# The x transposes of a chunked scan, one projection later

## Chip, cores and metric

One core of one Trainium2 chip runs the whole kernel as one program. The metric is device time in microseconds (us) for one execution; the kernel before takes 848.48 us (median of 3 runs, 846.72 to 849.82).

## What is computed

Two layers on 512 positions of width 1024, in float32: a bidirectional Mamba-2 (SSD) layer and a differential attention layer. The change lies in the SSD layer alone. Its scan, cut to what matters, with 8 groups of 4 heads of width 64, state 128, chunks of 128 positions (4 chunks), run forward and on the flipped sequence:

```python
X, B, C = chunks of (x * dt), B, C            # x, B, C: conv + SiLU of the input projection
L = exp(segment sums of dt * A)               # 128 x 128 per head, chunk and direction
y_diag = einsum(C, B, L, X)
states = einsum(B, exp(a_cs[-1] - a_cs), X)   # per chunk
prev   = running sum of states, decayed from chunk to chunk
y_off  = einsum(C, prev, exp(a_cs))
y = y_diag + y_off                            # both directions are summed; then + D * x, times SiLU(z)
```

## The kernel before

Each engine has its own program, written out by hand; they meet in counting semaphores, and each engine runs its own instructions in order. The SSD input projection is cut into units of 128 output channels. Six units (slots 0 to 5) make one iteration: z (two units), x (two units), B and C of one group. A unit is 24 matmuls of 512 columns (8 blocks of the inner dimension, three products each, since weights and activations are split into a high and a low part), made by `project` (L1288) into bank 0 or 1 in turn, so a projection waits for the SiLU of the unit two before it (L1292). Weights come by DMA into a ring of four buffers; ScalarE (ACT) rounds them to the high part (`split_hi`, L595) and GpSimd (POOL) takes the low part (`split_lo`, L469), three units ahead.

While the units of group g+1 are projected, the scan of group g is worked on between them; here "group g" names that iteration, and its steps in each slot are:

- slot 0: PE transposes x into banks 2 and 3 (8 transposes, L1307). ACT runs the tanh of z (L639), copies x to `x_nat` (two copies, L667) and does the exponentials of head 2 (L694). POOL does `split_lo`, then `scale_x_dec` (L487): two products of `x_nat` with the decays into `x_dec` (L493).
- slot 1: PE transposes B into bank 4 (L1317), makes C-by-B into bank 5 (L1320). ACT: tanh of z, copy of B (L685), exponentials of head 3, squares. DVE: SiLU of z (L952), then `pair_weights` (L958) for heads 0 and 1 and again for heads 2 and 3: two sums of rows, both inputs in SBUF (L962), then two products with bank 5 (L966).
- slot 2: PE makes the states from `x_dec` and `B_nat` into banks 4, 2 and 3 (L1331). DVE: convolution of x (L937, four taps), the running states (L976, L982), SiLU. POOL: `split_lo`, then `squares` (L511).
- slot 3: PE makes the diagonal part (L1342) and the part from earlier chunks (L1355). DVE: convolution, the y sums (L997 to L1006) into `x_nat`, SiLU. ACT issues the load of the next rows.
- slots 4 and 5: convolutions of B and C; POOL adds the masks (`mask_rows`, L504) for the next group; PE transposes y (L1362) after slot 5's projection.

PE does its scan work of a slot after that slot's projection. Groups 2 to 5 run in a hardware loop of two trips with two groups each. In the last group there are no units for slots 2 to 5; the first units of the output projection (`out_unit`, L1380) stand there, and DVE does two steps of the gate's low part (`gated_lo`, L1018, L1021; both inputs in SBUF) ahead of the SiLU of slot 1, for which the first `out_unit` waits (L1385).

Of the kernel before, what the change touches and what calls it, by code (L numbers as in the profile page):

```python
# [32 lines left out]
NC = L // P  # L33
# [8 lines left out]
GROUPS = 8  # L42
HPG = HEADS // GROUPS
# [80 lines left out]
def build(nc, x, norm_w, ssd_w_in, ssd_conv_w, ssd_conv_b, ssd_dt_bias, ssd_a_log, ssd_d,  # L124
# [3 lines left out]
    with stack:  # L128
# [202 lines left out]
        def after(eng, s, n):  # L331

            if not (isinstance(n, int) and n <= 0):
                eng.wait_ge(s, n)
# [104 lines left out]
        def _(pool):  # L439
# [74 lines left out]
            def ssd_iteration(m, half, slots=range(SLOTS), scan=True):  # L514
                last_g = isinstance(m, int) and m * 2 + half == GROUPS - 1
                for slot in range(SLOTS):
                    if slot == 0 and last_g:
                        scale_x_dec(GROUPS - 1)
                    if slot in slots:
                        split_lo(ssd_unit(m, half, slot).plus(AHEAD))  # L520
                    if scan and slot == 0 and not last_g:
                        if isinstance(m, int) and m * 2 + half == 0:
                            mask_rows(0, range(HPG))
                        scale_x_dec(m * 2 + half)
                    if scan and slot > 3 and slot in slots:
                        mask_rows(m * 2 + 1 + half, range(2 * slot - 8, 2 * slot - 6))
                    if scan and slot == 2 and not (isinstance(m, int) and m * 2 + half == 0):
                        squares(m * 2 + half - 1)
# [64 lines left out]
        def _(act):  # L593
# [64 lines left out]
                        .then_inc(sq_in, 1)  # L658

            def scan_ops(g, slot, half):  # L660
                if slot == 0:

                    after(act, y_done, g * NC)
                    after(act, yt_done, g * 2)
                    for i in range(2):
                        act.wait_ge(tr_done, g * 4 + i + 1)
                        nc.scalar.copy(x_nat[:, 2 * i:2 * i + 2, :].rearrange("p c w -> p (c w)"),  # L667
                                       bank[2 + i][:, :]).then_inc(x_nat_in, 1)
                last_g = isinstance(g, int) and g == GROUPS - 1
                if slot == 1 and not last_g:  # L670
                    copy_b(g)
                if slot == 2:
                    act.wait_ge(st_done, g * 3 + 1)
                    after(act, off_done, g * NC)
                    nc.scalar.copy(pair(0), bank[scan_banks(g)[0][0]][:, :]).then_inc(prev0_in, 1)
                first = isinstance(g, int) and g == 0
                for r in ((0,) if first else () if last_g else (2,),
                          (1, 2, 3) if first else (2, 3) if last_g else (3,), (), (), (), ())[slot]:
                    exps(g, r)

            def copy_b(g):

# [29 lines left out]
            def ssd_iteration(m, half, slots=range(SLOTS), scan=True):  # L712
                last_g = isinstance(m, int) and m * 2 + half == GROUPS - 1
                for slot in range(SLOTS):
                    if slot == 1 and last_g:
                        copy_b(GROUPS - 1)
                    if slot in slots:
                        split_hi(ssd_unit(m, half, slot).plus(AHEAD))
                        evacuate(m, half, slot)
                    if scan and slot == 5 and slot in slots:  # L720
                        exps(m * 2 + 1 + half, 0)
                    if slot == 1 and last_g:
                        gated_hi(0)
                        gated_hi(1)
                    if scan:
                        scan_ops(m * 2 + half, slot, half)
                    if scan and slot == 1 and not (isinstance(m, int) and m * 2 + half == 0):
                        squares(m * 2 + half - 1)
                    if slot in slots and slot >= 2:
                        tanh(m, half, slot)  # L730
                    if scan and slot == 3 and slot in slots:
                        load_rows(act, m * 2 + 1 + half)
                    if scan and slot == 5 and slot in slots:
                        exps(m * 2 + 1 + half, 1)
# [517 lines left out]
        def _(pe):  # L1252
# [44 lines left out]

            def scan_ops(g, slot, half):
                last_g = isinstance(g, int) and g == GROUPS - 1
                if slot == 0:  # L1300

                    pe.wait_ge(silu_done, g * SLOTS + 2)
                    after(pe, y_done, g * NC)
                    for i in range(2):
                        for c in (2 * i, 2 * i + 1):
                            for j in range(2):
                                ins = T.transpose(bank[2 + i][:, (c % 2) * GW + j * P:(c % 2) * GW + (j + 1) * P],  # L1307
                                                  xT[:, half, j, c * P:(c + 1) * P], ident[:, :])
                        ins.then_inc(tr_done, 1)
                if slot == 1:  # L1310

                    if isinstance(g, int) and g == 0:
                        pe.wait_ge(rows_sb, 1)
                        pe.wait_ge(sp_a, 7)
                    pe.wait_ge(silu_done, g * SLOTS + 4)
                    for c in range(NC):
                        ins = T.transpose(bank[4][:, c * P:(c + 1) * P], BT[:, c * P:(c + 1) * P], ident[:, :])  # L1317
                    ins.then_inc(tr_done, 1)
                    for c in range(NC):
                        ins = T.matmul(bank[5][:, c * P:(c + 1) * P], BT[:, c * P:(c + 1) * P],  # L1320
                                       CTr[:, c * P:(c + 1) * P], start=True, stop=True)
                    ins.then_inc(tr_done, 1)
                if slot == 2:

                    pe.wait_ge(xdec_done, g * 2 + 2)
                    pe.wait_ge(x_nat_in, g * 3 + 3)
                    after(pe, g_done, g * 2)
                    for k in range(3):
                        b = bank[scan_banks(g)[0][k]]
                        for d, (c, i) in enumerate(((k, k), (3 - k, 2 - k))):  # L1330
                            ins = T.matmul(b[:, d * GW:(d + 1) * GW], B_nat[:, c, :], x_dec[:, d, i, :],  # L1331
                                           start=True, stop=True)
                        ins.then_inc(st_done, 1)
                if slot == 3:

                    pe.wait_ge(m_done, g * HPG + HPG)
                    if last_g:
                        pe.wait_ge(prev_done, g + 1)
                    for c in range(NC):
                        for r in range(HPG):  # L1340
                            at = (c % 2) * GW + r * HD
                            ins = T.matmul(bank[6 + c // 2][:, at:at + HD], rows[:, r, c * P:(c + 1) * P],  # L1342
                                           x_nat[:, c, r * HD:(r + 1) * HD], start=True, stop=True)
                        if c % 2:
                            ins.then_inc(diag_done, 1)
                if slot == 3 or slot == 4 and last_g:

                    pe.wait_ge(prev_done, g + 1)
                    for c in (range(NC) if not last_g else range(2) if slot == 3 else range(2, NC)):
                        if slot == 4:  # L1350
                            pe.wait_ge(y_done, g * NC + c - 1)
                        for d in range(2):
                            k = (c - 1, 2 - c)[d]
                            if 0 <= k < 3:
                                ins = T.matmul(bank[scan_banks(g)[1][c]][:, d * GW:(d + 1) * GW], CTr[:, c * P:(c + 1) * P],  # L1355
                                               prev[:, k, d, :], start=True, stop=True)
                        ins.then_inc(off_done, 1)
                if slot == 5:
                    pe.wait_ge(y_done, g * NC + NC)
                    for j in range(2):  # L1360
                        for c in range(NC):
                            ins = T.transpose(bank[6 + j][:, c * P:(c + 1) * P], x_nat[:, c, j * P:(j + 1) * P],  # L1362
                                              ident[:, :])
                        ins.then_inc(yt_done, 1)
# [246 lines left out]
```

## Time and profile before

| | us |
|---|---|
| median of 3 runs | 848.48 |
| the profiled execution | 852.42 |
| its span in the trace | 850.7 |
| PE busy | 787.7 (93%) |
| DVE busy | 538.0 (63%) |
| POOL busy | 456.5 (54%) |
| ACT busy | 405.0 (48%) |
| mean granted TensorE clock | 0.982 of full speed |

All rows and numbers taken from the trace belong to the profiled execution, on a time axis that starts with its span. PE is the matmul side of TensorE, ACT is ScalarE, POOL is GpSimd, DVE is VectorE. Group 0 of the scan begins near 60 us, the following ones near 112, 157, 206, 252, 301, 347 and 392 us; the output projection and the attention layer follow.

### The profile page before, as it was taken

Reading aid. Unit: us, or ns where it says so; the run is one execution under the profiler, and the core shown is the slowest. Engines: PE = TensorE matmul, PEld = TensorE weight load, DVE = VectorE, ACT = ScalarE, POOL = GpSimd, SP = SyncE. Lnnn points to the kernel's source line nnn. Section 1 sums busy time; section 2 is a strip of 40 time slices with the busy share of each in tenths; the row PEclk is TensorE's granted clock in tenths of the full one; section 3 lists DMA queues with packets and bytes.
Section 4 is the critical chain, followed back from the end, with each engine's and each line's share of the span. In section 5 each row is a group of like instructions: output and inputs, shape, how many; then the busy total and the mean of one; then the engine's idle time right before and its main releaser. Section 6 shows DMA issues by size and latency. Waiting matters only on the chain.

```text
span 850.7 us, 11488 instructions
## 1 busy us (share of the span) xinstructions
PE 787.7 (93%) x3824; PEld 639.4 (75%) x3824; DVE 538.0 (63%) x893; ACT 405.0 (48%) x807; POOL 456.5 (54%) x254
## 2 busy tenths in 40 slices
PE   1987999999999899999799999899999999998887
PEld 0766888887878788888687888766777777776576
DVE  4754869596777859596662113367668677676732
ACT  4557273634637282745732134344645454645420
POOL 5438494856667475857545434645545636445111
PEclk9999899999999999999999999999999999999999
DMA  9115524324243424233152332513223132120002
GB/s 263 54 41 166 186 62 125 115 73 159 75 148 99 148 58 152 87 111 113 50 198 76 105 99 62 155 51 96 69 77 97 50 97 91 53 96 25 1 1 99
DMA packets 98804, 82.57 MB, mean 97 GB/s; under 512 B 5152, under 2 KB 87424, under 8 KB 96712
## 3 DMA queue, kind: packets, MB, share of 16 engines
q1 hardware_dynamic: 95760, 66.99, 26.4%
q10 hardware_dynamic: 2904, 15.01, 4.8%
q8 instruction: 24, 0.39, 0.2%
q14 instruction: 20, 0.16, 0.1%
q0 software_dynamic: 96, 0.02, 0.0%
HBM read 79.74 MB, written 2.26 MB: 96 GB/s over the span
## 4 chain that ended last, share of the span: by engine, by line
PE 51%; DVE 21%; issue 11%; POOL 8%; ACT 6%; DMA 1%; DVEq 1%; ACTq 0%; SPq 0%; POOLq 0%
PE bank L1259 42%; DVE c_acc L937 4%; POOL w_lo L472 3%; DVE rows L962 3%; POOL stat L464 2%; ACT ex L790 2%; PE bank L1342 2%; DVE sbias L1126 2%; PE bank L1331 1%; PE bank L1355 1%; POOL rows L504 1%; DVE tmp L997 1%; DVE ex L1137 1%; ACT qkvz L855 1%; ACT w_hi L601 1%
## 5 line engine op out<-in xcount | busy, mean ns | idle before, releaser
L472 POOL TENSOR_TENSOR w_lo<-w_raw,w_hi 128x1024 fp32r<-128x1024 f32 x104 | 260.9, 2510 | 256.4 <-ACT w_hi L601 256.3
L1259 PE MATMUL bank<-hn_hi,w_hi 128*128 128x512 f32 (+1 forms) x392 | 160.1, 408 | 11.1 <-DVE xT L952 7.7
L1259 PE MATMUL bank<-hn_hi,w_lo 128*128 128x512 f32 (+1 forms) x392 | 154.5, 394 | 0.0
L1259 PE MATMUL bank<-hn_lo,w_hi 128*128 128x512 f32 (+1 forms) x392 | 154.3, 394 | 0.0
L601 ACT CAST w_hi<-w_raw 128x1024 fp32r<-128x1024 f32 x104 | 108.8, 1047 | 77.1 <-PE bank L1259 70.7
L1259 PE MATMUL bank<-w_hi,hn_hi 128*128 128x512 f32 x320 | 131.4, 410 | 7.7 <-DVE zT L952 5.0
L1259 PE MATMUL bank<-w_hi,hn_lo 128*128 128x512 f32 x320 | 125.6, 392 | 0.0
L1259 PE MATMUL bank<-w_lo,hn_hi 128*128 128x512 f32 x320 | 125.6, 392 | 0.0
L937 DVE SCALAR_TENSOR_TENSOR c_acc<-bank,par,c_acc 128x510 f32<-128x510 f32 (+1 forms) x128 | 95.8, 748 | 34.1 <-ACT c_acc L643 25.4
L790 ACT ACTIVATE ex<-sbias,stat 128x512 f32<-128x512 f32 x64 | 45.7, 716 | 120.6 <-DVE stat L1130 120.6
L1259 PEld LDWEIGHTS bank<-hn_hi,w_hi 128*128 128x128 f32 (+1 forms) x392 | 74.2, 189 | 29.2 <-issue 14.0
L504 POOL TENSOR_TENSOR rows<-rows,below 128x1024 f32<-128x1024 f32 x32 | 76.5, 2415 | 21.3 <-DMA rows<-acs_rows 21.3
L1259 PEld LDWEIGHTS bank<-hn_hi,w_lo 128*128 128x128 f32 (+1 forms) x392 | 74.0, 189 | 16.7
L1259 PEld LDWEIGHTS bank<-hn_lo,w_hi 128*128 128x128 f32 (+1 forms) x392 | 74.2, 189 | 15.2
L1259 PEld LDWEIGHTS bank<-w_hi,hn_hi 128*128 128x128 f32 x320 | 60.5, 189 | 29.5 <-issue 13.3
L694 ACT ACTIVATE rows<-rows,da 128x128 f32<-128x128 f32 x256 | 78.0, 393 | 3.4 <-POOL rows L504 3.4
L650 ACT ACTIVATE bank<-c_acc 128x512 f32<-128x512 f32 x32 | 19.3, 602 | 115.9 <-DVE c_acc L937 115.9
L1259 PEld LDWEIGHTS bank<-w_hi,hn_lo 128*128 128x128 f32 x320 | 60.4, 189 | 13.3
L1259 PEld LDWEIGHTS bank<-w_lo,hn_hi 128*128 128x128 f32 x320 | 60.7, 190 | 11.0
L1259 PE MATMUL bank<-w_hi,oT_hi 128*128 128x512 f32 x128 | 53.2, 416 | 3.5 <-DVE stat L1130 1.6
L962 DVE TENSOR_TENSOR rows<-rows 128x512 f32<-128x512 f32 x32 | 49.8, 1590 | 3.0 <-ACT rows L694 3.0
L1259 PE MATMUL bank<-w_hi,oT_lo 128*128 128x512 f32 x128 | 51.6, 403 | 0.0
(191 smaller groups left out, 1265.1 us busy)
## 6 DMA issues: line engine op xcount, KB each, us to landing
w_raw<-in_ssd_w_in SPq DMA_DIRECT2D x48, 512.0 KB, 4.0
w_raw<-in_attn_w_in SPq DMA_DIRECT2D x64, 256.0 KB, 3.1
rows<-acs_rows ACTq DMA_DIRECT2D x14, 1024.0 KB, 6.4
w_raw<-in_ssd_w_out SPq DMA_DIRECT2D x16, 512.0 KB, 3.6
w_raw<-in_attn_w_out SPq DMA_DIRECT2D x16, 256.0 KB, 3.1
wbias<-bias_rows SPq DMA_DIRECT2D x8, 448.0 KB, 4.1
rows<-in_x SPq DMA_DIRECT2D x4, 512.0 KB, 5.4
rows<-acs_rows SPq DMA_DIRECT2D x2, 1024.0 KB, 5.9
```

Of the source, the lines that this page charges most:

```text
L464: return nc.gpsimd.tensor_tensor(dst, src, expo[:, 0:n], ALU.pow)
L472: nc.gpsimd.tensor_tensor(w_lo[:, s, :], w_raw[:, s, :], f32(w_hi[:, s, :]), ALU.subtract)\
L504: nc.gpsimd.tensor_tensor(pair_, pair_, below[:, :, :].unsqueeze(2).to_broadcast([P, 2, NC, P]), ALU.add).then_inc(mask_done, 1)
L601: nc.scalar.copy(w_hi[:, s, :], w_raw[:, s, :]).then_inc(hi_done, 1)
L650: nc.scalar.activation(bank[u.c % 2][:, :], c_acc[:, u.c % 2, :], ACT.Tanh).then_inc(tan_done, 1)
L694: ins = nc.scalar.activation(part, part, ACT.Exp, bias=da[:, c, d, ds(g * HPG + r, 1)])
L790: nc.scalar.activation(ex[:, j, :], sbias[:, j, :], ACT.Exp, bias=stat[:, 36 + j:37 + j], accum_out=stat[:, 40 + j:41 + j]).then_inc(e_don ...
L937: ins = V.scalar_tensor_tensor(c_acc[:, p, lo:hi], bank[p][:, lo + sh:hi + sh], par[:, ds(t + (PC_W + k * CT), 1)], c_acc[:, p, lo:hi], AL ...
L962: ins = V.tensor_tensor(rows[:, r, :], rows[:, r, :], rows[:, HPG + r, :], ALU.add)
L1126: ins = V.tensor_tensor_reduce(out=sbias[:, j, :], in0=bank[4 + j][:, :], in1=w, scale=1.0, scalar=-3.0e38, op0=ALU.add, op1=ALU.max, accu ...
L1259: ins = T.matmul(dst, a[i], b[j], start=first and n == 0, stop=last and n == 2)
L1342: ins = T.matmul(bank[6 + c // 2][:, at:at + HD], rows[:, r, c * P:(c + 1) * P], x_nat[:, c, r * HD:(r + 1) * HD], start=True, stop=True)
```

## The change

On PE, the eight x transposes of a group move from after slot 0's projection to after slot 1's projection, ahead of B's transposes. On ACT, the two copies of x move from slot 0 to slot 1, right ahead of the copy of B. On POOL, `scale_x_dec` stands at the beginning of slot 1 for all groups. For groups 0 to 6 that is the same place in POOL's order as before (behind slot 0's `split_lo`, ahead of slot 1's); in the last group it stood ahead of slot 0's `split_lo` and now stands behind it. In the last group ACT's copies of x stand with the copy of B ahead of slot 1's `split_hi` and tanh. No instruction is added or removed.

```diff
@@ POOL, ssd_iteration
-                    if slot == 0 and last_g:
-                        scale_x_dec(GROUPS - 1)
+                    if scan and slot == 1:
+                        scale_x_dec(m * 2 + half)
                     if slot in slots:
                         split_lo(ssd_unit(m, half, slot).plus(AHEAD))
-                    if scan and slot == 0 and not last_g:
-                        if isinstance(m, int) and m * 2 + half == 0:
-                            mask_rows(0, range(HPG))
-                        scale_x_dec(m * 2 + half)
+                    if scan and slot == 0 and isinstance(m, int) and m * 2 + half == 0:
+                        mask_rows(0, range(HPG))
@@ ACT, scan_ops
-                if slot == 0:
-
-                    after(act, y_done, g * NC)
-                    after(act, yt_done, g * 2)
-                    for i in range(2):
-                        act.wait_ge(tr_done, g * 4 + i + 1)
-                        nc.scalar.copy(x_nat[:, 2 * i:2 * i + 2, :].rearrange("p c w -> p (c w)"),
-                                       bank[2 + i][:, :]).then_inc(x_nat_in, 1)
                 if slot == 1 and not last_g:
+                    copy_x(g)
                     copy_b(g)
@@ ACT, new function with the lines removed above
+            def copy_x(g):
@@ ACT, ssd_iteration
                     if slot == 1 and last_g:
+                        copy_x(GROUPS - 1)
                         copy_b(GROUPS - 1)
@@ PE, scan_ops
-                if slot == 0:
+                if slot == 1:
 
                     pe.wait_ge(silu_done, g * SLOTS + 2)
                     after(pe, y_done, g * NC)
```

## Rows read from the trace of the kernel before

**Rows 1.** The page's chain that ended last: shares of the span by engine.
```profile
PE 51%; DVE 21%; issue 11%; POOL 8%; ACT 6%; DMA 1%; DVEq 1%; ACTq 0%; SPq 0%; POOLq 0%
```
**Rows 2.** Timeline of PE, groups 2 and 3: start, duration, engine, line, what [idle before].
```profile
162.88 1.03 PE L1307 MATMUL bank<-ident,xT 128*128 128x128 f32 x8
163.67 0.48 PE L1259 MATMUL bank<-hn_hi,w_hi 128*128 128x512 f32 x1
...
169.22 0.27 PE L1317 MATMUL bank<-ident,BT 128*128 128x128 f32 x1
...
198.03 0.47 PE L1259 MATMUL bank<-hn_hi,w_hi 128*128 128x512 f32 x1 [2.10 <-DVE xT L952]
...
245.90 0.47 PE L1259 MATMUL bank<-hn_hi,w_hi 128*128 128x512 f32 x1 [1.30 <-DVE xT L952]
```
**Rows 3.** Chain that ended last, in order of time: slot 5's projection in group 2.
```profile
198.03 7.31 PE bank L1259 x24
```
**Rows 4.** Busy time by window, columns PE, PEld, DVE, ACT, POOL, clock, DMA, GB/s.
```profile
200.00:202.00 2.00, 2.00 (x6) 1.62 (x5) 1.19 (x3) 0.74 (x2) 2.00 (x2) 0.50 0.01 2
```
**Rows 5.** Timeline of DVE, slot 1 of group 2, up to slot 2's convolution.
```profile
170.65 2.97 DVE L962 TENSOR_TENSOR rows<-rows 128x512 f32<-128x512 f32 x2
173.74 1.28 DVE L966 TENSOR_TENSOR rows<-rows,bank 128x512 f32<-128x512 f32 x2
...
174.95 2.90 DVE L962 TENSOR_TENSOR rows<-rows 128x512 f32<-128x512 f32 x1
...
180.76 0.74 DVE L937 SCALAR_TENSOR_TENSOR c_acc<-bank,par,c_acc 128x510 f32<-128x510 f32 x1
```
**Rows 6.** Timeline of DVE, the same stretch of group 3.
```profile
219.69 3.02 DVE L962 TENSOR_TENSOR rows<-rows 128x512 f32<-128x512 f32 x2
222.74 1.28 DVE L966 TENSOR_TENSOR rows<-rows,bank 128x512 f32<-128x512 f32 x2
...
223.94 0.68 DVE L962 TENSOR_TENSOR rows<-rows 128x512 f32<-128x512 f32 x1
...
228.62 0.74 DVE L937 SCALAR_TENSOR_TENSOR c_acc<-bank,par,c_acc 128x510 f32<-128x510 f32 x1
```
**Rows 7.** Timeline of POOL in slots 1 and 2 of groups 2 and 3.
```profile
170.08 2.39 POOL L472 TENSOR_TENSOR w_lo<-w_raw,w_hi 128x1024 fp32r<-128x1024 f32 x1
174.92 2.37 POOL L472 TENSOR_TENSOR w_lo<-w_raw,w_hi 128x1024 fp32r<-128x1024 f32 x1 [2.46 <-ACT w_hi L601]
...
223.94 2.90 POOL L472 TENSOR_TENSOR w_lo<-w_raw,w_hi 128x1024 fp32r<-128x1024 f32 x1 [2.39 <-ACT w_hi L601]
```
**Rows 8.** Timeline of ACT, tanh of slot 1 in group 3.
```profile
218.46 0.59 ACT L639 ACTIVATE c_tan<-bank 128x512 f32<-128x512 f32 x1
```
**Rows 9.** Timeline of ACT, slot 0 of the last group.
```profile
399.75 0.58 ACT L639 ACTIVATE c_tan<-bank 128x512 f32<-128x512 f32 x1
400.24 1.05 ACT L667 COPY x_nat<-bank 128x512 f32<-128x512 f32 x2
```
**Rows 10.** Timeline of POOL, slots 0 and 1 of the last group.
```profile
401.36 2.91 POOL L493 TENSOR_TENSOR x_dec<-x_nat,xdw 128x768 f32<-128x768 f32 x2 [1.69 <-ACT x_nat L667]
404.22 4.84 POOL L472 TENSOR_TENSOR w_lo<-w_raw,w_hi 128x1024 fp32r<-128x1024 f32 x2
```
**Rows 11.** Timeline of DVE in group 0, while POOL goes over to x_dec.
```profile
79.02 1.30 DVE L962 TENSOR_TENSOR rows<-rows 128x512 f32<-128x512 f32 x1 [1.51 <-ACT rows L694]
...
81.55 0.68 DVE L962 TENSOR_TENSOR rows<-rows 128x512 f32<-128x512 f32 x1
```
**Rows 12.** Timeline of POOL in group 0, the second x_dec product.
```profile
81.61 1.95 POOL L493 TENSOR_TENSOR x_dec<-x_nat,xdw 128x768 f32<-128x768 f32 x1
```
**Rows 13.** Timeline of DVE, slot 1 of the last group.
```profile
407.78 2.50 DVE L1021 SCALAR_TENSOR_TENSOR hn_lo<-gT,par,hn_hi 128x512 fp32r<-128x512 f32 x2 [6.73 <-ACT hn_hi L709]
```
**Rows 14.** Timeline of PE, first unit of the output projection.
```profile
410.93 0.80 PE L1259 MATMUL bank<-w_hi,hn_hi 128*128 128x512 f32 x1 [4.96 <-DVE zT L952]
```
**Rows 15.** Timeline of PE in group 0, the states.
```profile
83.62 0.79 PE L1331 MATMUL bank<-x_dec,B_nat 128*128 128x256 f32 x1 [3.75 <-POOL x_dec L493]
```

More of the change, by code:

```diff
@@ L679, in scan_ops @@
                     exps(g, r)
+            def copy_x(g):
+                after(act, y_done, g * NC)
+                after(act, yt_done, g * 2)
+                for i in range(2):
+                    act.wait_ge(tr_done, g * 4 + i + 1)
+                    nc.scalar.copy(x_nat[:, 2 * i:2 * i + 2, :].rearrange("p c w -> p (c w)"),
+                                   bank[2 + i][:, :]).then_inc(x_nat_in, 1)
             def copy_b(g):
```

## Prediction

> **What bounds the kernel now.** I read the page's chain first: PE carries half of it and DVE a fifth [rows 1]. In the SSD stage PE is nearly always busy, so the next question is where it isn't. The PE timeline answers: slot 5's projection waits for DVE's SiLU of x in the loop's groups, 2.10 us in group 2 and 1.30 in group 3 [rows 2]. The pattern repeats: groups 4 and 5 wait about 2.4 and 1.3; groups 1 and 6 wait next to nothing. A wait of 2.1 costs more than itself. The projection behind it has 7.31 us on the chain [rows 3], while an undisturbed one takes 169.22 - 163.67 = 5.55 [rows 2], and two microseconds after it began the granted clock is 0.50, the lower level of 1.2 GHz [rows 4]. After the wait of 1.30 no such stretch shows. I price the drop at 1.6 us (7.16 us to the next PE step less 5.55). So the even groups lose about 4 us each, the odd ones 1.3. PE further waits 3.75 us for `x_dec` in group 0 [rows 15] and 4.96 us for the SiLU of z in the last group [rows 14].
>
> Why is that SiLU late? DVE works without a break from the row sums of slot 1 on. A sum takes 0.68 us when it runs alone [rows 6], yet in group 2 the first two take 2.97 and the next 2.90 [rows 5]. The POOL timeline beside it shows why: `split_lo` runs from 170.08 to 172.47, and at 174.92, 0.03 us ahead of DVE's sum at 174.95 [rows 5, 7]. A sum with both inputs in SBUF thus stands still until POOL's running instruction is over, and ends 0.55 us later (170.65 + 2.97 less the second sum's 0.60 is 173.02, against 172.47). In group 3 both start at 223.94, DVE goes first in 0.68 us, and POOL's instruction stretches from 2.39 to 2.90 [rows 6, 7]. Whoever is first wins, and that is the difference between the even and the odd groups. From the first sum to slot 2's convolution: 180.76 - 170.65 = 10.11 us in group 2, 228.62 - 219.69 = 8.93 in group 3 [rows 5, 6].
>
> **PE, part by part.** The eight transposes take 163.67 - 162.88 = 0.79 us [rows 2] wherever they stand; PE's total is unchanged. But slot 1's projection now starts and ends 0.79 earlier. States need the products one projection (5.55 us) plus B and C-by-B later; POOL needs some 4.5 us, so no wait there. Slot 1's projection loses 0.79 us of slack on slot 5's SiLU of C; by my reading of the timelines 0.15 us is left in groups 3 to 5, so I take zero, and at most 0.2 us per group as a risk.
>
> **ACT.** Two copies take 1.05 us, 0.94 to the next start [rows 9]. In groups 3 to 5 the tanh of slot 1 shows no idle time ahead of it [rows 8]: ACT is late, not PE. Without the copies it starts 0.94 earlier; in groups 1 and 2 PE sets it, 0.79 earlier. In slot 1 the copies stand ahead of B's copy and head 3's exponentials, which end about 0.2 us later than now; DVE wants head 3 only with its fourth sum, three microseconds after that. Queued behind are the squares and slot 2's `split_hi`, whose reader POOL is busy anyway. No DMA of the ring is due within 15 us of it.
>
> **POOL and DVE: the race.** Count from slot 1's tanh, t = 0. Its SiLU ends such that the first sum starts at 1.22 (219.69 - 218.46) [rows 6, 8]. In the last group the copies follow the tanh at 0.49 and POOL starts `x_dec` at 1.61 [rows 9, 10]; I use that spacing. POOL meanwhile has nothing: its slot 0 `split_lo` is over, and the other waits behind `scale_x_dec`. So:
> - Sum 1 runs free, 1.22 to 1.90. POOL starts `x_dec` at 1.61, ahead of sum 2 (due at 1.82). One `x_dec` alone takes 1.46 [rows 10]; begun beside sum 1, about 1.6, so it ends at X = 3.2, and sum 2 ends at X + 0.55.
> - The two products follow after 0.03 (group 3) or 0.12 (group 2: 173.74 - 173.62) and take 1.20 [rows 5, 6]. Sum 3 is due at X + 1.78 in odd groups, X + 1.88 in even ones.
> - The second `x_dec` is stretched by the sum that was let in between. Group 0 shows this very pattern: sum waiting since 79.02, done at 80.32, next sum due at 81.55, second `x_dec` from 81.61 [rows 11, 12]; that is 1.88 us between the two `x_dec` starts. So slot 1's `split_lo` starts at X + 1.86.
> - Odd groups: sum 3 is 0.08 ahead, runs in 0.68 (as 81.55 did, 0.06 ahead [rows 11, 12]) and stretches `split_lo` to 2.90; sum 4 ends at X + 1.86 + 2.89 + 0.55 = X + 5.30, the convolution starts at X + 6.54 = 9.8, which is 8.55 behind sum 1 where it was 8.93.
> - Even groups: sum 3 is 0.02 late, waits for `split_lo` (2.39), and sum 4 for slot 2's `split_lo` right behind it. The convolution starts at X + 8.8 = 12.1, 10.85 behind sum 1 where it was 10.11.
>
> **Sum for the groups.** Groups 3 and 5: start 0.94 earlier, pair work 0.38 shorter, together 1.32; their wait of 1.30 goes: -2.6 in all. Groups 2 and 4: start 0.79 and 0.94 earlier, pair work 0.75 longer, together -0.1: waits and clock drops stay. Groups 1 and 6: DVE is earlier but no wait is there to take: 0. From the convolution on, everything moves with it.
>
> **Group 0.** POOL's four masks set `x_dec`, not the copies. ACT's exponentials of head 1 move behind the two copies, so DVE's second sum comes 0.9 us later, in the middle of the first `x_dec` and no longer ahead of it; that `x_dec` isn't stretched, states start 0.4 earlier: -0.4. PE then waits 0.8 more in slot 0 and less here. If the clock drop behind the 3.75 us wait [rows 15] shrinks too, -1.4 more at the outside; I take 0 for it.
>
> **Last group.** Now the copies wait for transposes behind slot 1's projection, so `x_dec` runs beside DVE's `gated_lo`, with `split_lo` behind it. Before, `gated_lo` waited once, for the second `split_lo` to end at 404.22 + 4.84 = 409.06, and took 2.50 for two [rows 10, 13]. Now: transposes from 403.7, copies to 405.4, `x_dec` 405.45 to 408.35, `split_lo` from 408.33. The first `gated_lo` ends near 408.95 and lets `split_lo` end only at 411.2; the second ends at 411.8 where it ended at 410.28. PE's 4.96 us wait grows by +1.5, fully on the path. Bounds: +0.2 if the second slips in between, +1.6.
>
> **Total:** -0.4 - 2.6 - 0.1 + 1.5 = -1.6 us of 852.42, so 850.8 for a profiled execution. That lies 3.9 above the median of 848.48; I take the difference off the median: 846.9.
>
> **A rule weighed.** By the row at 81.61 the waiting sum stretched the next `x_dec` by about 0.46, less than the 0.55 it took to finish, which puts POOL 0.02 ahead in even groups [rows 11, 12]. The Trainium skill, "SBUF — State Buffer", section "SBUF: two separate sides", calls the pair of ports an exclusive lock that the first holds for the whole instruction while the other fully blocks. Taken literally the stretch would be the full 0.55 and POOL's start X + 1.95, so sum 3 would be first in even groups too, and the time would be that of rival A. The trace agrees with the blocking, not with the full length.
>
> **Rivals.**
> A. *DVE wins in the even groups too.* The margin against it is 0.02 us, below what I can add up from rows; for it speaks the tie at 223.94, against it 174.95 lost by 0.03. Then groups 2 and 4 have their convolution 1.4 to 1.5 plus 0.79 to 0.94 earlier, the wait falls to 0.1 to 0.3, and the clock drop goes: 2 x (2.2 + 1.6) = 7.6 more, total -9.2: 839.3.
> B. *POOL wins everywhere (slower).* If `split_lo` starts 0.08 us earlier against sum 3 than I reckon, or the products 0.08 later, the odd groups lose as well. Pair work 10.85 in place of 8.93: +1.9 - 0.94 = +1.0. Groups 3 and 5 then wait 2.3, which brings the clock drop: 2 x (1.0 + 1.6) = +5.2; groups 1 and 6, which have almost no slack, +1.0 each; last group +1.5, group 0 and even groups -0.5: +8.2, 856.7. Against it stands group 0's precedent.
> C. *It moves nothing.* The earlier start is eaten by slot 5's SiLU of C, or another DVE wait takes over in slot 3: gains and the last group cancel, 0 to +1.5: 848.5 to 850.
>
> **Chances.** Forecast 0.42, A 0.28, B 0.13, C 0.12, the rest 0.05. A measurement can tell about 0.3%, 2.5 us, from no change. The forecast's own range is 844.5 to 848.5 (group 0's clock, last group's slip), so it is split, 0.17 faster and 0.25 same; A is faster, B slower, C mostly same. Faster 0.48, same 0.32, slower 0.20. The range reaches from 837.5 (A with part of group 0's clock) to 853, leaving out B and tails.
>
> **What would show it.** Right: sum 1 of slot 1 at 0.68 us in every group; `x_dec` between it and sum 2; odd groups' slot 5 without idle time; granted clock 0.50 left behind slot 5's wait in even groups; PE's wait in the last group near 6.5. Wrong: slot 3 of POOL or a wait of slot 1's projection for C in their place, or exponentials of head 3 as releaser of sum 4. The prediction hangs on who is first at sum 3: its duration, 0.68 or some 2.9, tells forecast, A and B apart.

## The result and the profile after

The change makes the kernel slower: 853.36 us (median of 12 runs, 850.40 to 856.07) against 849.72 for the kernel before in the same runs (12 runs, 846.40 to 852.39). The ratio is 1.0051, with a 95% interval of 1.0031 to 1.0071. The forecast was 846.9, a step of -1.6 us, with a range from 837.5 to 853.0. The measured step is +3.6 us by the medians.

The profiled execution doesn't show it at first sight. It took 851.72 us (span 850.0), less than the 852.42 of the one before. The first page lines after, to be read against [rows 1]:

```profile
PE 781.3 (92%) x3824; PEld 634.6 (75%) x3824; DVE 547.0 (64%) x893; ACT 405.3 (48%) x807; POOL 459.8 (54%) x254
...
PE 42%; DVE 27%; issue 12%; ACT 9%; POOL 8%; DMA 1%; DVEq 1%; ACTq 1%; SPq 0%; POOLq 0%
```
The chain has moved from PE (51 to 42%) to DVE (21 to 27%): DVE's lateness now reaches the end more often. Why is the span no longer, then? The code behind the scan is the same in both kernels, so I compare that stretch alone. Windows of the kernel before and of the one after, from the last group's y transposes to the end (columns: PE, PEld, DVE, ACT, POOL, granted clock, DMA share, GB/s):

```profile
443.76:850.70 406.94, 384.43 (x1841) 301.51 (x1839) 222.85 (x467) 174.79 (x328) 185.16 (x85) 0.98 0.24 73
```
```profile
446.52:850.00 403.48, 380.10 (x1841) 298.14 (x1839) 221.53 (x467) 174.72 (x328) 185.50 (x85) 1.00 0.24 74
```
The same work takes 406.94 us at a granted clock of 0.98 and 403.48 at 1.00. These 3.5 us belong to the two executions, not to the change. Up to the same mark, the last group's y transposes, the kernel after is 2.8 us later (446.52 against 443.76), and this too holds clock drops that fell here or there: between 60 us and the mark PE is idle for 22.0 us in place of 17.1, and busy for 364.5 us in place of 366.7 with the same matmuls, so drops that did not come take 2.2 us of it back. So the medians say how much, and the waits say where.

PE's waits after (timeline of PE; start, duration, what, and in brackets the idle time before and its releaser):

```profile
150.53 0.47 PE L1260 MATMUL bank<-hn_hi,w_hi 128*128 128x512 f32 x1 [1.19 <-DVE xT L953]
...
197.43 0.47 PE L1260 MATMUL bank<-hn_hi,w_hi 128*128 128x512 f32 x1 [1.94 <-DVE xT L953]
...
244.64 0.47 PE L1260 MATMUL bank<-hn_hi,w_hi 128*128 128x512 f32 x1 [2.19 <-DVE xT L953]
...
291.81 0.47 PE L1260 MATMUL bank<-hn_hi,w_hi 128*128 128x512 f32 x1 [2.24 <-DVE xT L953]
...
338.99 0.77 PE L1260 MATMUL bank<-hn_hi,w_hi 128*128 128x512 f32 x1 [2.27 <-DVE xT L953]
...
386.94 0.47 PE L1260 MATMUL bank<-hn_hi,w_hi 128*128 128x512 f32 x1 [1.38 <-DVE xT L953]
...
412.99 0.79 PE L1260 MATMUL bank<-w_hi,hn_hi 128*128 128x512 f32 x1 [6.36 <-DVE zT L953]
```
Slot 5's projection now waits in every group from 1 to 6. In groups 2 and 4 the wait is about what it was (1.94 and 2.24, against 2.10 [rows 2] and 2.38). In groups 3 and 5, where the forecast had none left, 1.30 became 2.19 and 2.27. Groups 1 and 6 wait 1.19 and 1.38, where it was nothing and 0.12. The last group's wait grew from 4.96 [rows 14] to 6.36.

**The race came out as forecast.** DVE after, the third row sum and the convolution in groups 2 and 3, and POOL's `split_lo` beside them:

```profile
173.23 2.92 DVE L963 TENSOR_TENSOR rows<-rows 128x512 f32<-128x512 f32 x1
...
180.14 0.74 DVE L938 SCALAR_TENSOR_TENSOR c_acc<-bank,par,c_acc 128x510 f32<-128x510 f32 x1
...
220.34 0.69 DVE L963 TENSOR_TENSOR rows<-rows 128x512 f32<-128x512 f32 x1
...
225.06 0.74 DVE L938 SCALAR_TENSOR_TENSOR c_acc<-bank,par,c_acc 128x510 f32<-128x510 f32 x1
```
```profile
173.20 2.40 POOL L472 TENSOR_TENSOR w_lo<-w_raw,w_hi 128x1024 fp32r<-128x1024 f32 x1
...
220.40 2.87 POOL L472 TENSOR_TENSOR w_lo<-w_raw,w_hi 128x1024 fp32r<-128x1024 f32 x1
```
In group 2 the sum asks 0.03 us behind POOL and takes 2.92; in group 3 it asks 0.06 ahead and takes 0.69. From slot 1's tanh to the convolution it is 12.04 us in group 2 and 9.75 in group 3, where the forecast said 12.1 and 9.8. Group 3's convolution does start earlier than it did. The gain is lost behind it.

**Where it is lost.** DVE's two running-state products of group 3 (both inputs in SBUF), before:

```profile
231.97 0.68 DVE L976 TENSOR_TENSOR tmp<-prev,dec 128x512 f32<-128x512 f32 x1
...
233.63 0.69 DVE L976 TENSOR_TENSOR tmp<-prev,dec 128x512 f32<-128x512 f32 x1
```
and after:

```profile
228.40 0.91 DVE L977 TENSOR_TENSOR tmp<-prev,dec 128x512 f32<-128x512 f32 x1
...
230.28 2.78 DVE L977 TENSOR_TENSOR tmp<-prev,dec 128x512 f32<-128x512 f32 x1
```
The second one takes 2.78 us in place of 0.69. POOL beside them, first before, then after:

```profile
228.71 1.30 POOL L511 TENSOR_TENSOR sq_acc<-sq_acc,sq 128x512 f32<-128x512 f32 x1 [0.16 <-POOL sq_acc L511]
...
233.73 2.80 POOL L472 TENSOR_TENSOR w_lo<-w_raw,w_hi 128x1024 fp32r<-128x1024 f32 x1 [3.73 <-ACT w_hi L601]
```
```profile
227.47 1.29 POOL L511 TENSOR_TENSOR sq_acc<-sq_acc,sq 128x512 f32<-128x512 f32 x1 [0.16 <-POOL sq_acc L511]
...
230.16 2.35 POOL L472 TENSOR_TENSOR w_lo<-w_raw,w_hi 128x1024 fp32r<-128x1024 f32 x1 [1.41 <-ACT w_hi L599]
```
Before, the last of POOL's squares sums was over at 230.01, some 2 us ahead of DVE's first product, and the second product came at 233.63, 0.10 us ahead of slot 3's `split_lo` at 233.73. After, the squares sum runs from 227.47 to 228.76, the first product asks at 228.40 and takes 0.91 in place of 0.68. So the second one asks at 230.28, and `split_lo` has begun at 230.16. It waits until POOL is done at 232.51. A delay of 0.2 us has lost a race and costs 2.1.

The cause is again in POOL's queue. `scale_x_dec` kept its place in the order but now waits for a later copy, and all that stands behind it comes later: two `split_lo` and then the two squares sums. I count from slot 1's tanh, which stands at 218.46 before [rows 8] and here after:

```profile
215.31 0.59 ACT L637 ACTIVATE c_tan<-bank 128x512 f32<-128x512 f32 x1
```
The first `split_lo` behind it starts 5.09 us after the tanh, where it was 0.68. The second starts at 7.92 in place of 5.48, and the last squares sum at 12.16 in place of 10.25. DVE's first running-state product has moved the other way, from 13.51 to 13.09. Slot 3's `split_lo` keeps its distance from the convolution (5.11 and 5.10 us), so it isn't what moved.

### The profile page after: what moved, and what is told of

It is laid out like the page before. It is cut to its first block, busy times and chain, and to the rows that moved or that the text cites. A ratio compares the mean times of both kernels' runs of the same rounds, so it can differ in the third digit from the quotient of the medians.

```text
span 850.0 us, 11484 instructions
## 1 busy us (share of the span) xinstructions
PE 781.3 (92%) x3824; PEld 634.6 (75%) x3824; DVE 547.0 (64%) x893; ACT 405.3 (48%) x807; POOL 459.8 (54%) x254
## 4 chain that ended last, share of the span: by engine, by line
PE 42%; DVE 27%; issue 12%; ACT 9%; POOL 8%; DMA 1%; DVEq 1%; ACTq 1%; SPq 0%; POOLq 0%
PE bank L1260 36%; DVE c_acc L938 6%; DVE rows L963 4%; POOL w_lo L472 3%; DVE tmp L977 2%; ACT ex L791 2%; POOL stat L464 2%; ACT rows L694 2%; ACT w_hi L599 2%; DVE sbias L1127 2%; DVE tmp L998 1%; PE bank L1343 1%; POOL rows L504 1%; DVE ex L1138 1%; ACT qkvz L856 1%
## 5 line engine op out<-in xcount | busy, mean ns | idle before, releaser
L472 POOL TENSOR_TENSOR w_lo<-w_raw,w_hi 128x1024 fp32r<-128x1024 f32 x104 | 263.6, 2539 | 236.5 <-ACT w_hi L599 236.5
L464 POOL TENSOR_TENSOR stat<-stat,expo 128x16 f32<-128x16 f32 (+1 forms) x16 | 31.3, 1954 | 36.6 <-DVE stat L1174 21.6
```

The source lines that it names most:

```text
L464: return nc.gpsimd.tensor_tensor(dst, src, expo[:, 0:n], ALU.pow)
L472: nc.gpsimd.tensor_tensor(w_lo[:, s, :], w_raw[:, s, :], f32(w_hi[:, s, :]), ALU.subtract)\
```

## The experiments

Each line has the kernel's median and that of the kernel before in the runs beside it.

| kernel | median us | before | ratio, 95% interval |
|---|---|---|---|
| last group put back | 850.85 | 849.55 | 1.0035 (1.0010 to 1.0060) |
| squares in slot 4 | 843.86 | 849.55 | 0.9952 (0.9929 to 0.9974) |
| squares thin | 843.99 | 849.55 | 0.9937 (0.9917 to 0.9957) |
| before, squares in slot 4 | 843.76 | 849.55 | 0.9941 (0.9921 to 0.9960) |
| both repairs | 842.47 | 847.92 | 0.9936 (0.9910 to 0.9961) |
| gap before slot 3's split_lo | 844.00 | 847.92 | 0.9956 (0.9932 to 0.9981) |
| both repairs and gap after x_dec | 837.02 | 847.92 | 0.9871 (0.9834 to 0.9909) |
| both repairs, split_lo first | 846.36 | 847.92 | 0.9974 (0.9946 to 1.0002) |

The theory has three parts: (1) the later `x_dec` pushes the squares onto the first running-state product, and the second then loses its race; (2) the last group pays by itself; (3) what keeps groups 2 and 4 late is the race for the third sum. The main rival is that DVE is late by the length of its pair sums alone, wherever the squares stand.

### The last group alone put back

```diff
@@ PE, scan_ops
-                if slot == 1:
+                if slot == (0 if last_g else 1):
@@ POOL, ssd_iteration
-                    if scan and slot == 1:
+                    if scan and slot == (0 if last_g else 1):
                         scale_x_dec(m * 2 + half)
@@ ACT, scan_ops
+                if slot == 0 and last_g:
+                    copy_x(g)
@@ ACT, ssd_iteration
-                        copy_x(GROUPS - 1)
                         copy_b(GROUPS - 1)
```

> The changed kernel with the last group alone put back: there the x transposes, copies and products stand in slot 0 as before. Theory (the last group pays by itself, because x_dec and split_lo now run one behind the other under DVE's two gated_lo): the first output unit's wait on the SiLU of z falls from 6.36 us to about 4.9, the time by 1.5 to 2.1 us against the changed kernel, so +1.5 to +2.5 against the kernel before. Groups 1 to 6 keep their slot-5 waits of 1.2 to 2.3 us. Rival (the stretch is bounded elsewhere): the wait goes and comes back at the states or the next unit, time stays at +3.7 to +4.3.

Measured: 850.85, 1.3 us above the kernel before by the medians and 2.5 less than the changed kernel's median (other runs, so to be taken with care). PE's wait in the last group, timeline of this kernel:

```profile
411.70 0.74 PE L1261 MATMUL bank<-w_hi,hn_hi 128*128 128x512 f32 x1 [4.96 <-DVE zT L954]
```
The wait is back at 4.96, and nothing takes its place. By the wait, part 2 holds. The time alone doesn't show it, since the step by ratio (1.0051 to 1.0035) is inside the intervals. It is the smaller part: the kernel is still slower than before by 0.1 to 0.6%, with the waits of 1.2 to 2.3 us in groups 1 to 6 unchanged.

### The squares moved, or made thin

```diff
@@ POOL, ssd_iteration
+                    if scan and slot == 4 and not (isinstance(m, int) and m * 2 + half == 0):
+                        squares(m * 2 + half - 1)
                     if scan and slot > 3 and slot in slots:
                         mask_rows(m * 2 + 1 + half, range(2 * slot - 8, 2 * slot - 6))
-                    if scan and slot == 2 and not (isinstance(m, int) and m * 2 + half == 0):
-                        squares(m * 2 + half - 1)
```

> The changed kernel with POOL's two squares sums moved from slot 2 to slot 4, behind its split_lo and ahead of the masks. Theory (the later x_dec pushes the squares onto the first running-state product, which then starts 0.2 us late and loses the second one's race against slot 3's split_lo): in groups 1, 3, 5 and 6 both running-state products of DVE take 0.68 us, where the second took 2.8; their slot-5 waits (1.2, 2.2, 2.3, 1.4) fall to 0 to 0.3. Groups 2 and 4 keep some 2 us of wait, since their sums 3 and 4 stand behind split_lo. Together 6 to 7 us off the changed kernel, -2 to -3 against the kernel before. Rival (the pair sums alone make DVE late): the waits stay and the time is +3.7 to +4.3. Bound for the side effect: a squares sum under the y sums of slot 3 or a mask 3 us later costs at most 0.5 us a group.

```diff
@@ POOL, squares
-                    nc.gpsimd.tensor_tensor(sq_acc[:, :], sq_acc[:, :], sq[:, j, :], ALU.add)
+                    nc.gpsimd.tensor_tensor(sq_acc[:, 0:8], sq_acc[:, 0:8], sq[:, j, 0:8], ALU.add)
```

> The changed kernel where POOL's squares sums take 8 of their 512 columns, so the gated norm's sum is not computed in full. It takes the suspected cost away without putting it elsewhere. Theory: the same as with the squares in slot 4 within 1 us (about -2 to -4 against the kernel before), running-state products at 0.68 us in all groups. Rival: no change, +3.7 to +4.3.

Measured: 843.86 and 843.99, both some 5 us under the kernel before, more than expected. With the squares in slot 4, the running-state products of group 3 and then all of PE's slot-5 waits over 0.3 us in groups 1 to 6:

```profile
225.42 0.68 DVE L977 TENSOR_TENSOR tmp<-prev,dec 128x512 f32<-128x512 f32 x1
...
227.07 0.69 DVE L977 TENSOR_TENSOR tmp<-prev,dec 128x512 f32<-128x512 f32 x1
```
```profile
194.44 0.47 PE L1260 MATMUL bank<-hn_hi,w_hi 128*128 128x512 f32 x1 [1.95 <-DVE xT L953]
...
286.76 0.47 PE L1260 MATMUL bank<-hn_hi,w_hi 128*128 128x512 f32 x1 [2.39 <-DVE xT L953]
...
377.14 0.47 PE L1260 MATMUL bank<-hn_hi,w_hi 128*128 128x512 f32 x1 [0.37 <-DVE xT L953]
```
Both products run free. Groups 1, 3 and 5 don't wait any more, group 6 waits 0.37, and groups 2 and 4 keep 1.95 and 2.39. That is the pattern that the forecast had drawn for the whole kernel. The thin squares give the same waits (1.96, 2.39, 0.45) and the same time, so it matters that the squares are gone from slot 2, and slot 4 costs nothing that shows. The rival has fallen: the pair sums weren't touched.

Part of the gain over the kernel before is not the waits. Behind the waits of 1.95 and 2.39 the projections take 5.72 and 5.69 us on the chain, where the kernel before has 7.31 [rows 3] and 7.33 behind 2.10 and 2.38. So some 3 us in this profile are clock drops that did not come. The mean granted clock of its twelve runs is 0.9905, that of the kernel before beside them 0.9859. Why the drops stayed away isn't shown; the section on the prediction comes back to it.

### The kernel before with the squares in slot 4

The same edit on the kernel before.

> The kernel before with nothing changed but POOL's squares sums in slot 4. Theory: in groups 2 and 4 sum 4 stood behind a squares sum (1.7 us); without it the pair work is 1.1 us shorter, the wait falls from 2.4 to 1.3 us, and with a wait of 1.3 the granted clock did not drop, so 2 x (1.1 + up to 1.6): -2 to -5.5 us against the kernel before. Groups 3 and 5 keep 1.3. Rival (the squares cost nothing where they stand, or the masks get late and take it back): 0 to +1.

Measured: 843.76, ratio 0.9941, at the wide end of the expected range. PE's slot-5 waits in groups 2, 3 and 4, then DVE's third and fourth sum of group 2 and the `split_lo` beside them:

```profile
196.88 0.47 PE L1259 MATMUL bank<-hn_hi,w_hi 128*128 128x512 f32 x1 [0.85 <-DVE xT L952]
...
243.14 0.47 PE L1259 MATMUL bank<-hn_hi,w_hi 128*128 128x512 f32 x1 [1.32 <-DVE xT L952]
...
289.50 0.47 PE L1259 MATMUL bank<-hn_hi,w_hi 128*128 128x512 f32 x1 [1.38 <-DVE xT L952]
```
```profile
174.90 3.46 DVE L962 TENSOR_TENSOR rows<-rows 128x512 f32<-128x512 f32 x2
```
```profile
175.03 2.78 POOL L472 TENSOR_TENSOR w_lo<-w_raw,w_hi 128x1024 fp32r<-128x1024 f32 x1 [2.61 <-ACT w_hi L601]
```
Group 4 falls from 2.38 to 1.38 as expected: its third sum still loses (2.85 us), but sum 4 no longer stands behind a squares sum and takes 0.68 in place of 1.77. Group 2 falls from 2.10 to 0.85 by something that I hadn't forecast. There the third sum asks 0.13 us ahead of `split_lo` and runs in 0.69 where it took 2.90 [rows 5], and sum 4 waits in its place. By ratio the squares' place is worth 0.6% without the moved transposes (0.9941) and 1.0% with them (1.0051 to 0.9952), and both kernels end at the same time within the intervals. The gain in the two tests above is thus not the changed kernel's own: with the squares in slot 4 the change alone is worth about nothing, and with them in slot 2 it costs.

### Only the race turned: a gap before slot 3's split_lo

The squares stay in slot 2. POOL gets one small product between slot 3's wait and its `split_lo`.

```diff
@@ build
+        pad = sb("pad", [P, 64])
@@ POOL, ssd_iteration
+                    if scan and slot == 3 and slot in slots:
+                        pool.wait_ge(hi_done, ssd_unit(m, half, slot).plus(AHEAD).u + 1)
+                        nc.gpsimd.tensor_tensor(pad[:, :], ones[:, 0:64], ones[:, 0:64], ALU.add)
                     if slot in slots:
                         split_lo(ssd_unit(m, half, slot).plus(AHEAD))
```

> The changed kernel, squares where they were, with one small product on POOL (128x64, into a scratch tile) between slot 3's wait for the high part and its split_lo. It takes nothing away; it only lets DVE's second running-state product, which asked 0.12 us too late in odd groups, be first. Theory (a lost race, not the length of the squares): the first product keeps its 0.9 us, the second falls from 2.8 to 0.7 to 0.9; slot-5 waits of groups 3 and 5 fall from 2.2 to 0.1 to 0.4, those of groups 1 and 6 from 1.2 and 1.4 to 0 to 0.4; about -6 us against the changed kernel, -1 to -3 against the kernel before. Rival (the squares cost by their own length): second product stays 2.8, or the waits stay; +3.5 to +5.

Measured: 844.00, ratio 0.9956. Group 3's two running-state products, POOL's small product beside them, and PE's slot-5 waits in groups 3, 4 and 5:

```profile
224.85 0.91 DVE L981 TENSOR_TENSOR tmp<-prev,dec 128x512 f32<-128x512 f32 x1
...
226.74 0.72 DVE L981 TENSOR_TENSOR tmp<-prev,dec 128x512 f32<-128x512 f32 x1
```
```profile
226.62 0.29 POOL L522 TENSOR_TENSOR pad<-ones 128x64 f32<-128x64 f32 x1 [1.41 <-ACT w_hi L603]
```
```profile
239.05 0.47 PE L1264 MATMUL bank<-hn_hi,w_hi 128*128 128x512 f32 x1 [0.20 <-DVE xT L957]
...
286.23 0.47 PE L1264 MATMUL bank<-hn_hi,w_hi 128*128 128x512 f32 x1 [2.25 <-DVE xT L957]
...
331.41 0.47 PE L1264 MATMUL bank<-hn_hi,w_hi 128*128 128x512 f32 x1 [0.16 <-DVE xT L957]
```
The first product still takes 0.91 under the squares sum. The second asks 0.12 us behind POOL as before, but now behind the small product, and falls from 2.78 to 0.72. The waits of groups 3 and 5 fall from 2.19 and 2.27 to 0.20 and 0.16, and those of groups 1 and 6 are gone. POOL has more to do than in the changed kernel and by the two ratios (1.0051 and 0.9956) the kernel is some 8 us faster than that one. So the squares' own length costs 0.2 us in groups 3 and 5 (0.5 in groups 1 and 6); the lost race behind it costs the rest. The size of the whole step, 8 us by ratio, is known to some 3 us. It is the cleanest of the tests, since nothing else is moved.

### Both repairs, and the gap behind x_dec

> The changed kernel with both repairs: squares sums in slot 4, last group put back. Theory (the two losses are separate and add up): slot-5 waits as with the squares moved (groups 2 and 4 near 2.0 and 2.4, the others 0 to 0.4), wait for the first output unit 4.9 us. 1.5 to 2 us below the changed kernel with the squares moved alone: -5 to -7 us against the kernel before. Rival (the last group's loss hides behind something once the groups are faster): -4.

Measured: 842.47. The waits are 1.94 and 2.39 in groups 2 and 4, 0.39 in group 6, and 4.96 in the last group: both repairs work side by side. By ratio the step from the squares alone (0.9952 to 0.9936) is as expected in size but inside the intervals.

To this, the gap that turns the even groups' race for the third row sum:

```diff
@@ POOL, ssd_iteration
                     if scan and slot == (0 if last_g else 1):
                         scale_x_dec(m * 2 + half)
+                        if not last_g:
+                            nc.gpsimd.tensor_tensor(pad[:, :], ones[:, 0:64], ones[:, 0:64], ALU.add)
```

> Both repairs, and the same small product on POOL between scale_x_dec and slot 1's split_lo. It turns the race for DVE's third row sum, which the even groups lose by 0.03 us. Theory: in groups 2 and 4 the third sum takes 0.7 to 0.9 us in place of 2.9, the convolution starts 9.9 to 10.1 us behind slot 1's tanh in place of 12.0, their slot-5 waits fall from 2.0 and 2.4 to 0 to 0.4, and no clock drop follows: another 4 to 7 us off, -9 to -12 against the kernel before. Rival (the even groups are late by something else in the loop): the waits stay, same as without the gap.

Measured: 837.02 (836.32 to 838.04), ratio 0.9871. Sums 3 and 4 of group 2 and the convolution behind them, POOL's small product and the `split_lo` behind it, then the only two slot-5 waits over 0.2 us in groups 1 to 6:

```profile
170.65 3.60 DVE L967 TENSOR_TENSOR rows<-rows 128x512 f32<-128x512 f32 x2
...
175.49 0.74 DVE L942 SCALAR_TENSOR_TENSOR c_acc<-bank,par,c_acc 128x510 f32<-128x510 f32 x1
```
```profile
170.62 0.29 POOL L521 TENSOR_TENSOR pad<-ones 128x64 f32<-128x64 f32 x1
170.87 2.83 POOL L473 TENSOR_TENSOR w_lo<-w_raw,w_hi 128x1024 fp32r<-128x1024 f32 x1
```
```profile
283.20 0.47 PE L1264 MATMUL bank<-hn_hi,w_hi 128*128 128x512 f32 x1 [0.28 <-DVE xT L957]
...
373.56 0.47 PE L1264 MATMUL bank<-hn_hi,w_hi 128*128 128x512 f32 x1 [0.39 <-DVE xT L957]
```
The two sums take 3.60 us where they took 5.68. Sum 4 begins at 171.38, so sum 3 was let in right behind the small product. The convolution starts 9.97 us behind the tanh (165.52). Groups 2, 3 and 5 don't wait; group 4 waits 0.28 and group 6 0.39. The odd groups gained too, which I hadn't forecast: in group 3 sum 3 is ahead of the small product, sum 4 behind it takes 0.78 us where it took 2.88, and the convolution comes 8.46 us behind the tanh in place of 9.75. There was next to no wait left to take there. This is rival A of the prediction, made by hand. It is the fastest version of the study, 1.3% under the kernel before. Whether the kernel before, with its transposes in slot 0, could be brought as far by another order wasn't tried.

### split_lo ahead of x_dec

```diff
@@ POOL, ssd_iteration (both repairs in place)
-                    if scan and slot == (0 if last_g else 1):
+                    if scan and slot == 0 and last_g:
                         scale_x_dec(m * 2 + half)
                     if slot in slots:
                         split_lo(ssd_unit(m, half, slot).plus(AHEAD))
+                    if scan and slot == 1 and not last_g:
+                        scale_x_dec(m * 2 + half)
```

> Both repairs, with POOL's slot 1 order turned: split_lo ahead of scale_x_dec (but for the last group). Theory: split_lo now meets sum 1 and x_dec sum 2, POOL has one instruction less under sums 3 and 4, so all groups alike start the convolution some 11.1 us behind slot 1's tanh (9.8 in odd, 12.0 in even groups without it): waits of 1.5 to 1.7 us in groups 2 to 5, none above 2. Against both repairs alone -1 to +2, so -3 to -7 against the kernel before. Rival (x_dec later makes the states late): PE waits for x_dec ahead of the states, +1 or more per group.

Measured: 846.36, ratio 0.9974: slower than expected, the interval reaches 1. Slot-5 waits in groups 2, 3 and 5, and the first two sums of group 3:

```profile
198.50 0.47 PE L1263 MATMUL bank<-hn_hi,w_hi 128*128 128x512 f32 x1 [0.66 <-DVE xT L956]
...
244.58 0.47 PE L1263 MATMUL bank<-hn_hi,w_hi 128*128 128x512 f32 x1 [1.12 <-DVE xT L956]
...
336.83 0.47 PE L1263 MATMUL bank<-hn_hi,w_hi 128*128 128x512 f32 x1 [1.14 <-DVE xT L956]
```
```profile
217.62 3.76 DVE L966 TENSOR_TENSOR rows<-rows 128x512 f32<-128x512 f32 x2
```
The waits are even lower than expected (0.66 and 1.1 to 1.2), though the first two sums take 3.76 us. What I had left out is group 0. There POOL is the bound, and a `split_lo` ahead of `x_dec` lets PE wait 5.22 us for the states, where both repairs show 2.40. These 2.8 us are most of the 3.9 between the two medians; what makes up the rest isn't shown. Only a part of the rival came true, in that one group.

## Why the prediction was wrong, point by point

- **What bounds the kernel**, PE but for DVE's late SiLU in slot 5, and the rule of who asks first: right.
- **ACT's relief and PE's 0.79 us**: right. In group 3 slot 1's tanh stands at 215.31, 0.45 us behind its projection's end (214.86); before it was 0.58 (218.46 against 217.88). The first sum runs free in groups 1 to 6.
- **The race for sum 3**: right in each of groups 1 to 6, with margins of 0.06 and 0.03 us where 0.08 and 0.02 were forecast. The prediction itself called 0.02 less than it could add up, so there is some luck in it. Rivals A and B, in which DVE or POOL wins everywhere, did not happen. B's waits (2.3 in groups 3 and 5, 1.0 in groups 1 and 6) came true all the same, by another cause.
- **"From the convolution on, everything moves with it"**: this step failed. DVE's chain moved earlier, POOL's squares moved later, and they met at the running states. From the convolution to slot 5's projection group 3 needed 245.90 - 228.62 = 17.28 us before [rows 2, 6] and 244.64 - 225.06 = 19.58 after. I had followed POOL's queue to slot 2's `split_lo` and stopped there, one instruction short. I had even named the squares among those "queued behind", but on ACT. Rival C held such a case ("another DVE wait takes over in slot 3"), priced at 0 to +1.5, without saying which wait or why. The sum put this term at nothing; it measured 19.58 - 17.28 = 2.3 us in group 3.
- **Groups 1 and 6 at 0**: wrong for the same reason, they wait 1.19 and 1.38. Against the forecast, groups 3 and 5 lost 2.2 us each and groups 1 and 6 some 1.3 each, 7 us in all; the median lies 6.5 above the forecast, of which 1.2 is that the kernel before itself came out at 849.72 in these runs and not at 848.48.
- **Last group, +1.5**: right. POOL's `x_dec` and `split_lo`, and DVE's two `gated_lo`:

```profile
406.13 2.90 POOL L493 TENSOR_TENSOR x_dec<-x_nat,xdw 128x768 f32<-128x768 f32 x2 [3.11 <-ACT x_nat L678]
408.99 2.80 POOL L472 TENSOR_TENSOR w_lo<-w_raw,w_hi 128x1024 fp32r<-128x1024 f32 x1
```
```profile
408.63 3.71 DVE L1022 SCALAR_TENSOR_TENSOR hn_lo<-gT,par,hn_hi 128x512 fp32r<-128x512 f32 x2 [6.88 <-ACT hn_hi L709]
```
  They take 3.71 us in place of 2.50 [rows 13]; the first waits for the second `x_dec`, the other for the stretched `split_lo`. PE's wait grows by 1.4.
- **Group 0, -0.4**: right, and by the mechanism named. The second sum comes at 80.00 in place of 79.02 [rows 11], the first `x_dec` takes 1.47 in place of 1.92, and the states start at 83.13, where it was 83.62 [rows 15]. The clock there was put at 0, with -1.4 at the outside; in this profile the outside value came true. The states and the projection behind them take 4.45 and 5.46 us on the chain, where it was 5.49 and 5.79.
- **The clock, 1.6 us for each wait over 2**: too sure. The kernel after has two such waits close together, the chain shows the projections behind them (groups 4 and 5):

```profile
291.81 5.70 PE bank L1260 x24
...
338.99 7.33 PE bank L1260 x24
```
  A wait of 2.24 us is followed by 5.70 us, one of 2.27 by 7.33. Of four waits between 1.94 and 2.27 one brought the drop. The other traces say the same: over the kernel before, this one and the experiments there are 18 slot-5 waits between 1.94 and 2.39 us, and five brought it. Behind 1.95 us the kernel with the last group put back has 7.35 us on the chain, and the one with the squares in slot 4 has 5.72; 2.38 brought the drop in the kernel before, 2.39 in none of three kernels. So it isn't the length of the wait alone. What decides isn't shown. The rest of the forecast doesn't depend on it, since it left the even groups' drops where they were, but rivals A and B were priced too high by it.
- **The rule weighed** (the Trainium skill, "SBUF — State Buffer", "SBUF: two separate sides"): the Trainium skill has the first one hold the pair of ports while the other fully blocks, and DVE's waits agree with it. The sum that asks at 173.23 ends 0.55 us after POOL's `split_lo`, and so does the product that asks at 230.28. The literal reading, by which DVE would win in the even groups, does not come out: the second `x_dec` is stretched by 0.45 us (1.92 in place of 1.47), not by the full 0.55, and sum 3 lost there by 0.03 us.

The sum of waits agrees in sign and roughly in size with the measured +3.6 us of the medians (by ratio 4.3, with an interval of 2.6 to 6.0): +0.9 and +1.0 in groups 3 and 5, +1.2 and +1.3 in groups 1 and 6, -0.2 and -0.1 in the even groups, +1.4 in the last, -0.5 in group 0, together +4.9. Clock drops don't add to it: the mean granted clock is 0.987 over the twelve runs of the kernel after and 0.986 over the 64 runs of the kernel before that stand beside the experiments.

## What to carry to other kernels

When an instruction is made to wait longer on an in-order engine, follow that engine's queue until it is idle again, and lay each instruction that moved beside those of the engine that it takes turns with, as POOL and DVE's instructions with two SBUF inputs do here. In this kernel 0.1 us of timing became 2 us of waiting, so a schedule's worth hangs on who asks first; count such places before counting work. Bulk work that nobody waits for, as a running sum of squares, belongs where the other engine does nothing of the kind, and a tiny instruction ahead of a long one can be enough to let the other go first.

## What the runs showed of the hardware

That a small POOL product (0.29 us) makes the kernel faster by 5 us was not in my mind when I made the prediction (842.47 to 837.02, medians on the same chip). DVE's sum asked 0.03 us behind it, waited for it, and went ahead of the 2.4 us `split_lo` that POOL had next. That the granted clock falls behind one wait of 1.95 us and not behind one of 2.39 was not expected either.
